# Retention on one core: values centred as they leave PSUM, mean squares in place of moments, output parts summed on TensorE

## The reference, cut to what matters

```
inner = einsum('bnihd,bnjhd->bnhij', qc, kc) * decay          # chunks of 128 tokens, 4 heads of 64
inner = einsum('bnhij,bnjhe->bnihe', inner, vc)
cross = einsum('bnihd,nbhde->bnihe', qc, prev_states) * xi
o = inner + cross
mu  = mean(o over the head's 64 columns)
var = mean((o - mu)**2)
o = (o - mu) * rsqrt(var + eps) * gn_w + gn_b
return silu(g) * o
```

## Time and the profile before

| what | before |
|---|---|
| median of 3 runs | 2645.51 us (2643.24 to 2648.67) |
| profiled execution, its own time | 2646.41 us |
| its span, first to last instruction | 2644.6 us |
| TensorE busy | 2555.4 us, 97% |
| VectorE busy | 1531.2 us, 58% |
| ScalarE busy | 1095.3 us, 41% |
| GpSimd busy | 1013.6 us, 38% |
| mean granted TensorE clock | 0.992 |

### The profile page before, as it was taken

The page is one execution under the profiler, slowest core; times in us unless marked ns, Lnnn a source line. Parts: engine busy times, 40 slices in busy tenths (PEclk is TensorE's granted clock), DMA queues, the critical chain, the costliest instruction groups (busy, mean ns, idle before and its releaser), DMA issues. The chain is left out here.

```text
span 2644.6 us, 43326 instructions
## 1 busy us (share of the span) xinstructions
PE 2555.4 (97%) x13188; PEld 2191.1 (83%) x13188; DVE 1531.2 (58%) x3045; ACT 1095.3 (41%) x2503; POOL 1013.6 (38%) x1161
## 2 busy tenths in 40 slices
PE   7999989999999999999999999999999999999997
PEld 6999977878788888888889998777887888888886
DVE  4667555472654455577647775555627454545785
ACT  4444554372522332344444455444634232223444
POOL 2455422174254545201044555222723545451012
PEclk8999999999999999999999999999999999999999
DMA  5111011014233233573321101012222233327533
GB/s 182 29 34 35 20 38 39 28 66 152 68 108 114 80 115 107 181 264 96 104 100 33 46 19 42 5 39 86 87 86 91 85 112 110 100 91 261 195 97 122
DMA packets 238651, 242.68 MB, mean 92 GB/s; under 512 B 27904, under 2 KB 171008, under 8 KB 238464
## 3 DMA queue, kind: packets, MB, share of 16 engines
q1 hardware_dynamic: 238464, 240.43, 28.1%
HBM read 172.75 MB, written 67.63 MB: 91 GB/s over the span
## 5 line engine op out<-in xcount | busy, mean ns | idle before, releaser
L2470 POOL TENSOR_TENSOR fw_a_lo<-fw_a_raw,fw_a_hi 128x512 fp32r<-128x512 f32 x132 | 178.8, 1355 | 457.6 <-DVE fw_s_raw L2053 457.6
L2470 POOL TENSOR_TENSOR fw_s_lo<-fw_s_raw,fw_s_hi 128x512 fp32r<-128x512 f32 x176 | 230.9, 1324 | 53.6 <-ACT fw_s_hi L1543 53.6
L733 PE MATMUL banks<-ht_hi,da_hi 128*128 128x512 f32 x496 | 193.2, 390 | 0.0
L733 PE MATMUL banks<-ht_lo,da_hi 128*128 128x512 f32 x496 | 193.2, 390 | 0.0
L733 PE MATMUL banks<-ht_hi,da_lo 128*128 128x512 f32 x496 | 193.2, 390 | 0.0
L733 PE MATMUL banks<-w_diff_hi,ht_hi 128*128 128x384 f32 x512 | 181.2, 354 | 6.1 <-DVE ht_lo L1730 4.1
L733 PE MATMUL banks<-w_diff_hi,ht_lo 128*128 128x384 f32 x512 | 173.5, 339 | 0.0
L733 PE MATMUL banks<-w_diff_lo,ht_hi 128*128 128x384 f32 x512 | 173.2, 338 | 0.0
L2298 POOL TENSOR_TENSOR qk_rot<-rope_a,rope_b 128x512 f32<-128x512 f32 x64 | 82.7, 1292 | 204.1 <-DVE rope_b L1759 204.1
L1787 DVE TENSOR_REDUCE stats<-banks 128x1 f32<-128x1024 f32 (+3 forms) x192 | 138.5, 749 | 29.3 <-PE banks L944 23.4
L1617 ACT ACTIVATE u_two<-u_two 128x512 f32<-128x512 f32 x42 | 26.6, 632 | 281.7 <-DVE u_two L2164 281.7
(11 more groups left out here) (357 smaller groups left out, 7506.8 us busy)
## 6 DMA issues: line engine op xcount, KB each, us to landing
da_raw<-act_scratch SPq DMA_DIRECT2D x154, 256.0 KB, 2.7
fw_a_raw<-in_w_gate_dram SPq DMA_DIRECT2D x88, 256.0 KB, 3.1
act_scratch<-act_s SPq DMA_DIRECT2D x66, 256.0 KB, 3.0
w_diff_raw<-in_w_in_dram SPq DMA_DIRECT2D x24, 512.0 KB, 6.4
fw_a<-in_w_up_dram SPq DMA_DIRECT2D x44, 256.0 KB, 3.2
fw_a_raw<-in_w_up_dram SPq DMA_DIRECT2D x44, 256.0 KB, 2.9
act_scratch<-act_zero SPq DMA_DIRECT2D x44, 256.0 KB, 2.4
act_scratch<-act_one SPq DMA_DIRECT2D x44, 256.0 KB, 2.8
```

The lines of the kernel that those rows point to most:

```text
L733: mm = pe.matmul(bank, lhsT, rhs, start=first and i == 0, stop=last and i == len(pairs) - 1, skip_group_check=resumes)
L2470: pool.tensor_tensor(w[1][:], w[2][:], w[0][:].bitcast(F32), ALU.subtract).then_inc(S["f_lo"], 1)
```

## The change

Five things change together.

1. `ret_take_z` (ScalarE) empties the bank in four copies: 256 columns of q and k; 64 columns of v for each head, scaled by the decay and with their sum accumulated into `v_sum`; 128 columns of the gate.
2. `ret_rotate` (VectorE) no longer scales v; with one instruction of the same width it subtracts a 64th of the sum, so that v is centred.
3. `ret_output` (TensorE) uses `split`: three products of 64 columns per head and source, all into the same 64 columns. It issues 12 products where there were 8, and 6 where there were 4 in the first chunk of a pair; the columns that stream through are the same in number.
4. `ret_take` is a plain copy on ScalarE. `bn_stats`, `bn_aggr` and `ret_offset` are gone. ScalarE squares two units at once (`ret_squares`), VectorE sums the squares (`ret_sums`), makes the mean squares (`ret_mean_squares`) and scales both units by the inverse root in one instruction (`ret_normed`), which ScalarE did before in two per unit.
5. GpSimd's `ret_root` loses its addition, and `ret_finish` of pair m is issued at step 2m + 7 where it stood at 2m + 9.

```diff
@@ TensorE, ret_output
-                    def both_parts(j, hi, lo, sides, first, last):
-                        pe.matmul(banks[:, RET_OUT[j], 0:P].rearrange("p (c d) -> p c d", c=2), hi, sides, start=first, stop=False)
-                        return pe.matmul(banks[:, RET_OUT[j], 0:64], lo, sides[:, 0, :], start=False, stop=last)
-
                     for j in range(2):
-                        mm = both_parts(j, r_at_hi[n % 2][:, tokens(j)], r_at_lo[n % 2][:, tokens(j)], rv[n % 5][:, j], True, t == 0)
+                        mm = products(ret_rows(j), split((r_at_hi[n % 2][:, tokens(j)], r_at_lo[n % 2][:, tokens(j)]),
+                                                            (rv[n % 5][:, j, 0, :], rv[n % 5][:, j, 1, :])), last=t == 0)
                     if t >= 1:
...
-                            mm = both_parts(j, rt_hi[n % 3][at_, 0, :], rt_lo[n % 3][at_, 0, :], state[at_, :, at_], False, True)
+                            mm = products(ret_rows(j), split((rt_hi[n % 3][at_, 0, :], rt_lo[n % 3][at_, 0, :]),
+                                                                (state[at_, 0, at_], state[at_, 1, at_])), first=False)
@@ ScalarE
-                def ret_normed(n):
...
+                def ret_take(n):
+                    m = n // 2
+                    act.wait_ge(S["ro_done"], L * PER["ro_done"] + n + 1)
+                    if m >= 3:
+                        act.wait_ge(S["r_on"], L * PER["r_on"] + m - 2)
+                    act.activation(r_sum[m % 3][:, n % 2], banks[:, RET_OUT[0]:RET_OUT[1] + 1, 0:RET_DIM], ACT.Copy).then_inc(S["r_take"], 1)
+
+                def ret_squares(m):
+                    act.wait_ge(S["r_take"], L * PER["r_take"] + 2 * m + 2)
+                    if m >= 1:
+                        act.wait_ge(S["r_ss"], L * PER["r_ss"] + m)
+                    act.activation(r_square[:], r_sum[m % 3][:], ACT.Square).then_inc(S["r_sq"], 1)
 
                 def ret_take_z(a):
                     if a in ret_unit_at:
                         n = ret_unit_at[a]
                         act.wait_ge(S["z_done"], L * PER["z_done"] + Z_RET + n + 1)
-                        act.activation(r_z[n][:], banks[:, Z_BANK, :], ACT.Copy).then_inc(S["z_free"], 1)
+                        act.activation(r_z[n][:, 0:2 * P], banks[:, Z_BANK, 0:2 * P], ACT.Copy)
+                        for j in range(2):
+                            v = slice(2 * P + RET_DIM * j, 2 * P + RET_DIM * (j + 1))
+                            act.activation(r_z[n][:, v], banks[:, Z_BANK, v], ACT.Copy, scale=xz[:, n // T, j:j + 1], accum_out=v_sum[:, n, j:j + 1])
+                        act.activation(r_z[n][:, 3 * P:4 * P], banks[:, Z_BANK, 3 * P:4 * P], ACT.Copy).then_inc(S["z_free"], 1)
@@ VectorE
-                    dve.tensor_tensor(v, v, xz[:, n // T, 0:2].unsqueeze(2).to_broadcast([P, 2, RET_DIM]), ALU.mult)
+                    dve.scalar_tensor_tensor(v, v_sum[:, n, :].unsqueeze(2).to_broadcast([P, 2, RET_DIM]), -1.0 / RET_DIM, v, ALU.mult, ALU.add)
...
-                def ret_take(n):
-                def ret_moments(n):
...
+                def ret_sums(m):
+                    dve.wait_ge(S["r_sq"], L * PER["r_sq"] + m + 1)
...
+                    dve.tensor_reduce(r_ss[:, m % 2], r_square[:], AX_X, ALU.add).then_inc(S["r_ss"], 1)
...
                 for u in RET_STEPS:
-                    if 0 <= u - 3 < RET_UNITS:
-                        ret_take(u - 3)
+                    m = u // 2 - 2
+                    if u % 2 == 1 and 0 <= m < RET_UNITS // 2:
+                        ret_sums(m)
                     if u < RET_UNITS:
                         ret_low(u)
+                    if u % 2 == 1 and 0 <= m < RET_UNITS // 2:
+                        ret_mean_squares(m)
                     if 0 <= u - 1 < RET_UNITS:
                         ret_inner(u - 1)
-                    if 0 <= u - 3 < RET_UNITS:
-                        ret_moments(u - 3)
-                    if u >= 6 and u % 2 == 0 and u // 2 - 3 < RET_UNITS // 2:
-                        ret_offset(u // 2 - 3)
+                    if u % 2 == 0 and 0 <= m - 1 < RET_UNITS // 2:
+                        ret_normed(m - 1)
@@ GpSimd
-                    if u >= 9 and u % 2 == 1 and u != RET_UNITS - 1:
-                        ret_finish((u - 9) // 2)
-                    if u == RET_UNITS:
-                        ret_finish((u - 10) // 2)
+                    if u >= 7 and u % 2 == 1 and (u - 7) // 2 < RET_UNITS // 2:
+                        ret_finish((u - 7) // 2)
```

More of the change, by code:

```diff
@@ L304, in hybrid_block_kernel @@
     r_sum = [sb(f"r_sum{i}", [P, 2, 2, RET_DIM], F32, EREG + (12 + i) * KB) for i in range(3)]
+    r_square = sb("r_square", [P, 2, 2, RET_DIM], F32, EREG + 15 * KB)
     r_st2 = [sb(f"r_st2{i}", [P, 2, P], F32R, HT + (29 + i) * KB) for i in range(3)]
@@ L415, in hybrid_block_kernel @@
     m_rs = small(2, T)
[L416 to L420, removed]
+    v_sum = small(2 * T, 2)
+    r_ss = small(2, 2, 2)
+    r_rs = small(2, 2, 2)
+    r_ms = small(2, 2, 2)
     minus_half = small(4)
@@ L448, in hybrid_block_kernel, with ret_rows @@
         RET_INNER, RET_STATE, RET_OUT = (0, 1), 7, (2, 3)
+        def ret_rows(j):
+            return banks[:, RET_OUT[j], 0:RET_DIM]
         def tokens(t, n=1):
@@ L1517, in _ @@
                 for u in RET_STEPS:
+                    if 0 <= u - 3 < RET_UNITS:
+                        ret_take(u - 3)
                     if u < RET_UNITS:
@@ L1522, in _ @@
                         ret_gate_and_v(u + 2)
-                    if 0 <= u - 7 < RET_UNITS:
-                        ret_normed(u - 7)
                     if 0 <= u - 1 < RET_UNITS:
                         ret_inner(u - 1)
+                    if u % 2 == 0 and 0 <= u // 2 - 2 < RET_UNITS // 2:
+                        ret_squares(u // 2 - 2)
                     if u in ROUND_OUT:
@@ L1965, in ret_inner @@
                         st.then_inc(S["r_st"], 1)
-                def ret_take(n):
[L1968 to L1973, removed]
-                def ret_moments(n):
[L1976 to L1985, removed]
+                def ret_sums(m):
+                    dve.wait_ge(S["r_sq"], L * PER["r_sq"] + m + 1)
+                    if m >= 2:
+                        dve.wait_ge(S["r_ms"], L * PER["r_ms"] + m - 1)
+                    dve.tensor_reduce(r_ss[:, m % 2], r_square[:], AX_X, ALU.add).then_inc(S["r_ss"], 1)
                 def ret_state_low(n):
@@ L1993, in ret_state_low, with ret_mean_squares, ret_normed @@
                                                  ALU.mult, ALU.subtract).then_inc(S["r_stlo"], 1)
-                def ret_offset(m):
+                def ret_mean_squares(m):
+                    b, p = m % 2, 2 * m // T
+                    dve.wait_ge(S["r_ss"], L * PER["r_ss"] + m + 1)
+                    if m >= 2:
+                        dve.wait_ge(S["r_rstd"], L * PER["r_rstd"] + m - 1)
+                    dve.scalar_tensor_tensor(r_ms[:, b], r_ss[:, b], 1.0 / RET_DIM, xz[:, p, 2:4].unsqueeze(1).to_broadcast([P, 2, 2]),
+                                             ALU.mult, ALU.add).then_inc(S["r_ms"], 1)
+                def ret_normed(m):
                     b = m % 2
@@ L1998, in ret_offset @@
                     if m >= 2:
-                        dve.wait_ge(S["r_on"], L * PER["r_on"] + 2 * (m - 1))
-                    dve.scalar_tensor_tensor(r_nb[:, b, :], mv[:, b, :, 0], -1.0, r_rs[:, b, :], ALU.mult, ALU.mult).then_inc(S["r_nb"], 1)
+                        dve.wait_ge(S["r_mx"], L * PER["r_mx"] + m - 1)
+                    dve.tensor_tensor(r_norm[b][:].rearrange("p i (j d) -> p i j d", j=2), r_sum[m % 3][:],
+                                      r_rs[:, b].unsqueeze(3).to_broadcast([P, 2, 2, RET_DIM]), ALU.mult).then_inc(S["r_on"], 1)
                 for a in MLA_STEPS:
```

18 lines of the change are left out of this document (7 added, 11 removed).

## The result

The changed kernel takes 2701.32 us in the median (2697.48 to 2702.81, 4 runs), the kernel before 2647.06 (2643.24 to 2648.67, 4 runs): ratio 1.0205, 95% interval 1.0190 to 1.0220, so about 54 us slower. The forecast was 2654.4 with a range up to 2664. Its direction held, its size did not: of the 54 us it had priced about 9.

What follows compares the result with a forecast made beforehand. It took TensorE to bound the kernel, full in the MLA stage and with gaps in retention. Products 10.1, less gaps 5.6, plus bank release 4.4 gave +8.9 us on 2646.41: 2655.3, median 2654.4, range 2645.5 to 2664.

Steps and rivals of the forecast that it cites:

- the moved `ret_finish`: GpSimd's queue at step 7: `rk_lo` of step 8 ready about when wanted; cost nothing, up to 1 us a layer.
- an `issue` gap at steps 7 to 9: Profile sign that the forecast is wrong: retention-stage gaps naming GpSimd or an `issue` at those steps; no size given.
- rival of gaps that come back around step 7: Retention stage: products cost 10.1 us, waits stay, now for GpSimd and VectorE; +14.5 us, 2660.0, chance 0.17.
- The added products: TensorE's retention output: 46 serial places a layer at 0.11 us, 5.1 us a layer, 10.1 in both.
- rival of free products: Retention output: second load of the same weights hides under the stream before; -1.2 us, 2644.3, chance 0.13.
- The bounds that I gave for a place: Price of one added serial product on TensorE in retention: 0.06 to 0.15 us, so 5.5 to 13.8 us.
- The gaps given back: Retention stage: five TensorE waits per layer behind VectorE and GpSimd vanish; 2.8 us a layer, 5.6 in both, 0 to 7.0.
- VectorE's and ScalarE's new instructions: Retention stage: both engines stay below TensorE, so these edits cost nothing on the path.
- not under 30: Profile sign that the forecast is right: VectorE busy under 30 of 40 us in the retention stage.
- The bank release: MLA stage: `z_free` rises 0.61 us later, TensorE's next projection waits; 2.2 us a layer, 4.4 in both.

Runs made afterwards that it cites:

- f3_no_split_hidden: Changed kernel with eight output products, `ret_finish` at its old steps, bank released behind one 512-column copy, v scaled and summed afterwards from SBUF: 2676.07 us, ratio 1.0101.
- e1_more_fill: Changed kernel with one more empty 512-column product ahead of the output products in every retention step: 2663.6 us, ratio 1.0066.
- f2_before_late: Kernel before, with GpSimd making output weights 5, 6 and 7 all at step 7, so `rk_lo` comes late: 2654.68 us, ratio 1.0052.

## Why the prediction was wrong

**The step that failed** is the moved `ret_finish`: "Four instructions more stand in that queue before something that TensorE waits for. By my count along the queue this `rk_lo` is ready about when it is wanted, so I cost it at nothing and keep up to 1 us a layer". The place and the mechanism were named, but the size was wrong twice. The wait was 1.7 us from start to start against a regular 0.2, so 1.5 us and not about nothing. The four instructions take 2.6 us; without them `rk_lo` would have been ready some 1.1 us ahead of time (an estimate: 1898.75 - 2.6 = 1896.15 against 1897.2), and 2.6 - 1.1 is the wait. The step from unit 8 to unit 9 lasts only 2.95 us on TensorE, since unit 7, the last chunk of its pair, makes no state product; I had written of 3.53 for a step, which accounts for 0.6 of the 1.5. And the sum had no term for the clock that a wait can cost: that term is some 23 us a layer. One step later in the queue, and the time is 2653.3, within 1.1 us of the forecast. The prediction's sign for this, an `issue` gap at steps 7 to 9, is there, and its rival of gaps that come back around step 7 names the place, but prices it at 5.6 us in all.

**The clock.** In the changed kernel the two pieces of the retention stage grow by 26.3 and 25.8 us a layer; in the kernel with `ret_finish` half way by 1.5. The difference, 24.7 and 24.3, is the price of 51.2 us at half clock together with the wait of 1.5 us; the half clock alone is 23.2 and 22.8. The Trainium skill, page "TensorE: Matmul & The Clock Gate", section "HAM oscillation — how this bites in real kernels", tells of matmuls broken up by waits for DMA, behind which each group starts at the low clock, and prices this as the throttled time by one minus the ratio of the clocks. By that rule 51.2 us would cost 25.6, an estimate; the trace agrees to about a tenth, with 23.2 and 22.8. No such case stood among my rivals, though the kernel's own empty products are there to keep the clock: a stage that carries them says that the clock is at risk in it.

**The added products** were right in price. A step went from 3.20 to 3.53 us, three serial places of 0.11, as forecast. The rival of free products falls. (The bounds that I gave for a place, 0.06 and 0.15, were misread: the starts in the earlier trace rows give 0.05 to 0.17.)

**The gaps given back** were right in kind and too small. The stage and what follows it grow by 1.5 us a layer with the clock held; 46 x 0.11 = 5.06 for the products less 1.52 makes 3.5 returned, where I took 2.8 and named 3.5 as the upper end. TensorE's 40.00 of 40.00 shows that none is left. With twelve products VectorE's and ScalarE's new instructions are hidden, as I said, though VectorE is at 33.59 of 40 us, not under 30.

**The bank release** was right, in kind and in size. ScalarE in the changed kernel, and the weight load behind it:

```profile
479.96 0.38 ACT L1496 ACTIVATE r_z<-banks 128x256 f32<-128x256 f32 x1 [1.96 <-PE banks L737]
480.24 0.31 ACT L1499 ACTIVATE r_z<-banks,stats 128x64 f32<-128x64 f32 x1
480.44 0.20 ACT L1499 ACTIVATION_READ_ACCUMULATOR r_z<-banks,stats 128x1 f32 x1
480.53 0.31 ACT L1499 ACTIVATE r_z<-banks,stats 128x64 f32<-128x64 f32 x1
480.73 0.21 ACT L1499 ACTIVATION_READ_ACCUMULATOR r_z<-banks,stats 128x1 f32 x1
480.82 0.28 ACT L1500 ACTIVATE r_z<-banks 128x128 f32<-128x128 f32 x1
...
481.16 0.19 PEld L737 LDWEIGHTS banks<-w_ret_hi,ht_hi 128*128 128x128 f32 x1 [0.80 <-ACT r_z L1500]
```

The release comes 481.10 - 479.96 = 1.14 us after the first copy starts, 0.54 later than the 0.60 of the earlier trace rows; I had 0.61. It cost 1.8 to 2.0 us a layer in the MLA piece where I had 2.2. Six loads of the next projection in a layer come 0.05 us behind the release, where two did before. These waits make 1.6 to 1.7 us a layer; the rest arises between the projections of units 7 and 8, where no load waits for the bank. The kernels with the early release give only 1.25 back, and what they keep, some 0.5 us, lies in that same stretch; its cause is not shown.

Put together for the kernel that holds its clock: 2 x 1.5 in the retention stage, 2 x 1.8 in the MLA stage, 0.5 between them make 7.1 us, against my 8.9 and a measured difference of medians of 7.8.

**What stays open.** Of the falls in kernels with twelve products, all nine that the profiled executions show last until 2.5 to 6.6 us before the last output product, whichever step they start at. With eight products those that start at step 9 end by step 11, but the two that start at step 11 (f3_no_split_hidden) last until 3.1 and 5.7 us before the last output product as well, and I have no experiment that separates the place from the two waits ahead of them. Nor is it settled which waits bring a fall: two of 1.02 and 1.04 us at the same place of e1_more_fill went either way, and the length of the half clock differs between runs of one kernel (f2_before_late: 2652.5 to 2687.3 us). The kernel before stands near this edge itself: it has waits of 0.98 and 1.00 us from load to load at step 11 without a fall, and 11 of its 98 runs took 2663 to 2669 us at a mean clock of 0.982 to 0.984, where most have 0.990 to 0.995. No profile of such a run was kept.

## What to carry to other kernels

When an instruction moves ahead in an engine's queue, lay out that queue and the other engine's steps around the new place with the durations of the rows, each step with its own length; "about when it is wanted" is a wait of unknown size. In a stage where TensorE is full only with many small products, price a wait of a microsecond or more twice: once as itself, and once, as the upper end, as the rest of the stage at half clock (here 1.5 and some 23 us a layer). And if a change costs far more than its parts, look first at the granted clock by window, then at the last wait ahead of its fall.

## What was not expected of the hardware

- A single wait of 1.7 us, in a stage in which TensorE is otherwise full, went with 51.2 us at half clock, in both layers; without the wait there was none.
- Two causes, the narrow products and the late `rk_lo`, that cost 5.4 and 9.6 us by themselves cost 55.9 together.
- An empty product of 512 columns more per step made the changed kernel 38 us faster.
- At half clock a step of 3.53 us took 6.34, a factor of 1.80 and not 2.
- An accumulating copy of 64 columns out of PSUM took 0.31 us, hardly less than the 0.38 for 256 columns without a sum.
